# Router, token gather, expert tail and norms rebuilt in a two-block float32 kernel on one core

## What is computed

```python
def expert_choice_ffn(h, w_router, w1, w3, w2):
    cap = EC_CAPACITY_FACTOR * N // N_EXPERTS          # 32 tokens for each of 16 experts
    aff = jax.nn.softmax((h @ w_router).astype(jnp.float32), axis=-1)
    gate, idx = lax.top_k(jnp.swapaxes(aff, 1, 2), cap)
    xg = h[bidx, idx]
    ye = jnp.einsum('becf,efd->becd', jax.nn.silu(a) * b, w2) * gate[..., None]   # a, b = xg @ w1, xg @ w3
    return jnp.zeros_like(h).at[bidx, idx].add(ye)

hx2 = modulate(rmsnorm(x, norm_ffn_g[l]), ada_x[3], ada_x[4])
x = x + ada_x[5][:, None, :] * expert_choice_ffn(hx2, w_router[l], w_exp1[l], w_exp3[l], w_exp2[l])
return rmsnorm(x, final_norm_g)                        # the second block starts with a norm of this
```

## Time and profile before

| | us |
|---|---|
| median of 3 runs (lowest 2255.99, highest 2257.81) | 2257.02 |
| the profiled execution's own time | 2254.84 |
| its span, first to last instruction | 2253.0 |
| PE busy | 1889.1 |
| VectorE busy | 744.3 |
| ScalarE busy | 334.6 |
| PE starts expert 0 | 414.81 |
| PE starts the last expert's last tile | 1319.93 |
| PE starts `in0_0` of the second block | 1341.29 |

### The profile page before, as it was taken

One profiled execution on the slowest core, in us unless ns is written; L12 is line 12 of the kernel. 1 busy time (PEld: TensorE's weight loads), 2 busy tenths in 40 slices (PEclk: granted clock), 3 DMA queues, 4 the chain that ended last, 5 costly groups with the idle time before them and its releaser, 6 DMA issues.

```text
span 2253.0 us, 29442 instructions
## 1 busy us (share of the span) xinstructions
PE 1889.1 (84%) x12382; PEld 1264.7 (56%) x12382; DVE 744.3 (33%) x1716; ACT 334.6 (15%) x759; POOL 0.2 (0%) x4
## 2 busy tenths in 40 slices
...
GB/s 327 114 210 239 224 254 357 405 428 428 428 429 428 429 428 428 428 428 428 428 428 429 428 377 168 186 75 164 230 168 183 186 179 183 76 168 241 152 169 57
DMA packets 148022, 648.82 MB, mean 288 GB/s; under 512 B 10660, under 2 KB 17425, under 8 KB 123158
## 3 DMA queue, kind: packets, MB, share of 16 engines
...
HBM read 646.36 MB, written 1.05 MB: 287 GB/s over the span
## 4 chain that ended last, share of the span: by engine, by line
PE 59%; DMA 33%; DVE 4%; ACT 2%; issue 1%; SPq 0%; ACTq 0%; DVEq 0%
DMA ring<-in_w_exp 33%; PE bank L2086 15%; PE bank L922 13%; PE bank L2769 6%; PE bank L1869 4%; PE bank L1606 4%; PE bank L2684 3%; PE bank L1884 2%; PE bank L936 1%; PE bank L965 1%; PE bank L800 1%; PE bank L1533 1%; DVE scr L2595 1%; PE bank L963 1%; PE bank L451 1%
## 5 line engine op out<-in xcount | busy, mean ns | idle before, releaser
L1869 PE MATMUL bank<-ring,arena 128*32 128x512 f32 x1968 | 305.2, 754 | 207.9 <-DMA ring<-in_w_exp 197.5
L1869 PEld LDWEIGHTS bank<-ring,arena 128*32 128x32 f32 x1968 | 60.9, 124 | 433.4 <-DMA ring<-in_w_exp 313.5
L922 PE MATMUL bank<-hx,ring 128*128 128x256 f32 x1344 | 293.0, 379 | 0.7 <-ACT hx L818 0.7
L922 PEld LDWEIGHTS bank<-hx,ring 128*128 128x128 f32 x1344 | 254.6, 190 | 37.5 <-issue 3.4
L1884 PE MATMUL bank<-ring,arena 128*32 128x512 f32 x1008 | 161.0, 781 | 78.9 <-DMA ring<-in_w_exp 67.9
L1927 DVE COPY arena<-bank 128x256 f32<-128x256 f32 x16 | 6.8, 425 | 527.2 <-PE bank L1874 527.2
L2086 PE MATMUL bank<-arena 128*128 128x256 f32 x672 | 151.0, 379 | 0.2 <-DVE arena L2135 0.2
L1884 PEld LDWEIGHTS bank<-ring,arena 128*32 128x32 f32 x1008 | 32.9, 132 | 188.7 <-DMA ring<-in_w_exp 107.8
L2086 PEld LDWEIGHTS bank<-arena 128*128 128x128 f32 x672 | 127.0, 190 | 17.5 <-DVE arena L2135 0.6
L1934 DVE COPY arena<-bank 128x256 f32<-128x256 f32 x16 | 6.8, 424 | 344.6 <-PE bank L1758 344.6
L2086 PE MATMUL bank<-ring,hx 128*128 128x256 f32 x448 | 105.8, 379 | 0.0
...
## 6 DMA issues: line engine op xcount, KB each, us to landing
ring<-in_w_exp SPq DMA_DIRECT2D x186, 2048.0 KB, 16.3
...
```

The costliest lines, as they stand in the source:

```text
L922: ins = pe.matmul(b[:, o:o + n], w[:, k, j * P:(j + 1) * P], h[:, k, :], start=k == 0, stop=k == KD - 1)
L1869: ins = pe.matmul(banks[s][32 * j:32 * j + 32, :], e_xe[:, 2 * t + kk, :], w[:, kk, 512 * j:512 * j + 512], start=t + kk == 0, stop=t + kk ...
```

## The change

1. **Four more later tiles on VectorE**: 6, 8, 10 and 12 join 0 to 5 (two within Hyena, two within the mLSTM heads).
2. **late-2 and late-1 leave the router.** All pairs move down: layer one of the second block now has -2 (behind `in0_0`), -1 (within attention), 0 (behind attention), 1 (in the norm); layer two has 2 to 5 alike, with 2 in its first norm. No pair stands in the join.
3. **Router.** Logits are taken from `xT` with the gain multiplied into `w_router`, half of them within `mixout`; the token's scale is applied later, to 16 logits and to the turned rows. The token's sum of squares comes from matmuls that use the squares as weights and move 2 columns of ones; VectorE adds six of the eight blocks first. `pe_rope` and the shift's part move into `mixout`.
4. **Gather.** `e_htok` is now the weights (128 columns, every second element) and `e_ps` moves, so that the result is already turned; copy and turn go. VectorE adds the shift on the way to `e_xe`.
5. **Expert 0's tiles.** 4 to 7, 10 and 11 are in the extra places, 0 to 3 in the ring, 8 and 9 follow as 0 and 1 are used, and expert 1's first four as 2, 3, 8 and 9 are used.
6. **The last expert** leaves the loop: no gather, its last tile in two halves, each half of `y` copied as it is done, and `x moe` by pairs as the scatter goes on.
7. **Join and norms**: the sum of squares is per token (weights: squares; two columns of ones move), root and reciprocal are of 128x2, and a diagonal matrix brings the scale back over partitions (`pe_scale`). For the final norm of block one the squares are folded to two blocks, and it is done after `in0_0` (`pe_fin`).

```diff
-    tiles("late-2_", later[16:18])
-    tiles("late-1_", later[18:20])
...
+        tiles2(f"late{g}_", later[20 + 2 * g:22 + 2 * g] if g < 0 else late[2 * g:2 * g + 2])
...
-    ON_DVE = 6
+    ON_DVE = (0, 1, 2, 3, 4, 5, 6, 8, 10, 12)
     later_acc = [arena[:, 14368 + 512 * i:14880 + 512 * i].rearrange("p (a b) -> p a b", a=2) for i in range(2)]
     later_acc += [hcx[:, 2 * i:2 * i + 2, 0:N] for i in range(4)]
+    later_acc += [later_acc[2 + n // 2] for n in range(8)]
...
+    def pe_late(pe, g, between=None):
...
+            if between and i == 0:
+                between(pe)
...
         def pe_norm(pe):
             PE.stage("norm")
             b = bank(pe, key)
             for k in range(KD):
                 pe.wait_ge(*at(f"{key} square{k}"))
-                ins = pe.matmul(b[:, 0:n], ones[:, 0:P], sq[:, k, :], start=k == 0, stop=k == KD - 1)
+                for c in range(NC):
+                    ins = pe.matmul(b[:, 2 * c:2 * c + 2], sq[:, k, c * P:(c + 1) * P], ones[:, 0:2], start=k + c == 0, stop=True,
+                                    skip_group_check=True)
             ins.then_inc(*PE.step(f"full {key}"))
 
-        def act_squares(act):
+        def pe_scale(pe):
+            stage = PE.cur
+            PE.stage("norm")
+            b = bank(pe, f"{key} scale")
+            for c in range(NC):
+                pe.wait_ge(*at(f"{key} diagonal{c}"))
+                ins = pe.matmul(b[:, c * P:(c + 1) * P], ones[:, 0:P], n_diag[:, c, :], start=True, stop=True)
+            ins.then_inc(*PE.step(f"full {key} scale"))
...
+            act.activation(n_root, bank_of(key)[:, 0:4:2], ACT.Sqrt, bias=n_eps, scale=1.0 / D).then_inc(
...
+            v.reciprocal(n_rs, n_root).then_inc(*DV.step())
             v.wait_ge(*DV.last())
+            for c in range(NC):
+                v.tensor_scalar(n_diag[:, c, :], ident[:, :], n_rs[:, c:c + 1], None, ALU.mult).then_inc(
+                    *DV.step(f"{key} diagonal{c}"))
...
+    def pe_fin(pe):
+        PE.stage("join")
+        pe.wait_ge(*at("fin squares"))
+        b = bank(pe, "join x")
+        for k in range(2):
+            ins = pe.matmul(b[:, 0:N], ones[:, 0:P], sqx[:, k, :], start=k == 0, stop=k == 1)
+        ins.then_inc(*PE.step("full join x"))
...
+            if h in (0, 2):
+                dve_later_sum(v, 10 + h, 0)
+                dve_later_sum(v, 10 + h, 1)
...
+            dve_later_sum(v, 6 + 2 * o, 0)
+            dve_later_sum(v, 6 + 2 * o, 1)
...
+    EXTRA = [(4, view(arena, 0, P, TILE)), (5, view(arena, 4096, P, TILE)), (6, view(arena, 8192, P, TILE)),
+             (7, view(arena, 12288, P, TILE)), (10, mg[:, :]), (11, scr[:, :])]
     extra_of = dict(EXTRA)
-    ring_of = {t: N_PRE + m for m, t in enumerate((5, 6, 7, 8, 10, 11))}
+    ring_of = {t: N_PRE + m for m, t in enumerate((0, 1, 2, 3, 8, 9))}
...
+        elif j == 1:
+            pe_rope(pe)
+        elif j == 5:
+            pe_route_logits(pe, 0)
...
     def pe_gather(pe, name):
 
-        for c in range(NC):
-            for j in range(4):
-                ins = pe.matmul(banks[2][32 * j:32 * j + 32, 0:256], e_ps[:, c, :], e_htok[:, c, 256 * j:256 * j + 256],
-                                    start=c == 0, stop=c == NC - 1)
+        for t in range(4):
+            for kk in range(2):
+                o = banks[2][:, (2 * t + kk) * CAP:(2 * t + kk + 1) * CAP]
+                for c in range(NC):
+                    ins = pe.matmul(o, e_htok[:, c, 256 * t + kk:256 * (t + 1):2], e_ps[:, c, :], start=c == 0, stop=c == NC - 1)
         ins.then_inc(*PE.step(f"{name}gathered"))
 
-    def pe_gather_turn(pe, name):
-
-        for kk in range(2):
-            ins = pe.transpose(banks[2][:, 256 + kk * P:256 + (kk + 1) * P], e_gx[:, kk::2], ident[:, :])
-        ins.then_inc(*PE.step(f"{name}turned"))
+    def dve_gathered(v, name):
+
+        v.wait_ge(*at(f"{name}gathered"))
+        v.tensor_tensor(e_xe, banks[2][:, 0:256].rearrange("p (k s) -> p k s", k=KD), spread(e_shp, 2, CAP), ALU.add).then_inc(
+            *DV.step(f"{name}xe"))
...
+                if last and t == 3:
+                    pe.wait_ge(K.sem("tile_half"), 16)
+                    w = place(EXP0 + 11, P, 4, D)
+                else:
+                    w = tile(8 + t, 4, D)
                 for half in range(2):
+                    if last and t == 3 and half:
+                        tile(11, 4, D)
...
+                pe.wait_ge(*at("last G"))
+                for j in range(KD):
+                    pe.wait_ge(*at(f"last y{j // 4}"))
+                    ins = pe.matmul(banks[4 + j // 2][:, (j % 2) * N:(j % 2 + 1) * N], e_y[:, j * P:(j + 1) * P], e_G,
+                                        start=False, stop=True, skip_group_check=True)
+                    ins.then_inc(*PE.step(f"last scattered{j}"))
+                return
...
+                if l == 0 and t == 0:
+                    pe_fin(pe)
+                    pe_late(pe, 4 * l - 2)
+                    PE.stage("second")
...
+        pe_late(pe, 4 * l - 1)
...
         sp.wait_ge(*at("z2"))
-        extra_tile(0)
-        extra_tile(1)
+        extra_tile(4)
+        extra_tile(5)
         sp.wait_ge(*at("full merge07"))
-        one(N_PRE - 4, stream[N_PRE - 4])
-        one(N_PRE - 3, stream[N_PRE - 3])
-        extra_tile(2)
-        extra_tile(3)
+        extra_tile(6)
+        extra_tile(7)
         sp.wait_ge(*at("merged0 done7"))
-        extra_tile(4)
-        one(N_PRE - 2, stream[N_PRE - 2])
-        one(N_PRE - 1, stream[N_PRE - 1])
-        for t in (5, 6):
+        extra_tile(10)
+        for t in (0, 1, 2, 3):
             sp.wait_ge(*at(f"used {ring_of[t] - RING}"))
             expert_tile(ring_of[t], 0, t)
-        sp.wait_ge(*at("h ffn0 done"))
-        extra_tile(9)
-        for t in (7, 8):
-            sp.wait_ge(*at(f"used {ring_of[t] - RING}"))
-            expert_tile(ring_of[t], 0, t)
+        sp.wait_ge(*at("full token sums"))
+        extra_tile(11)
         K.turn = 0
-        for t, old in ((10, 5), (11, 6)):
+        for t, old in ((8, 0), (9, 1)):
             sp.wait_ge(*at(f"expert used{old}"))
             expert_tile(ring_of[t], 0, t)
-        for t, old in enumerate((7, 8, 10, 11)):
+        for t, old in enumerate((2, 3, 8, 9)):
...
+        sp.dma_start(place(n, P, 4, D)[:, :, 0:512], w[:, :, 0:512]).then_inc(K.sem("tile_half"), 16)
+        sp.dma_start(place(n, P, 4, D)[:, :, 512:1024], w[:, :, 512:1024]).then_inc(tile_sem(n), 16)
...
```

500 lines of the change are left out of this document (314 added, 186 removed).

## The result

The changed kernel takes 2263.67 us (median of 12 runs, 2259.62 to 2268.61) against 2256.11 for the kernel before (12 runs, 2254.61 to 2259.26) on the same chip: ratio 1.0031, 95% interval 1.0023 to 1.0039. It is slower by 7.6 us; 2241.2 was forecast, with 0.05 on this side. The profiled execution took 2264.78, its span is 2262.7. PE is busy 1957.0 us, 68 more than before, though four tiles of `w_ada` have gone from it to VectorE.

A forecast was written before the change was run, and what follows sets the result against it. DMA of expert weights sets the experts' pace; most of the rest is PE. Gains of 11.0 us up to expert 0, 2.6 stream and 9.9 tail, less 7.7 second block, make 15.8: 2241.2 us, range 2236 to 2247.

The forecast's parts named there:

- Step 3: Expert weight stream: the last half starts 902.5 us after expert 0's start, a gain of 2.6 us.
- the gather starves the ring: Expert loop: DMA runs dry if gather and scatter exceed 14 us; 12 us of gather would give 2271; chance 0.05.
- Step 2: Router chain from the end of `mixout` to expert 0: 19 us; expert 0 starts at 403.8, 11 us earlier.
- Step 1: First block: four later tiles on VectorE and earlier branch tiles bring the merges 5.6 us earlier (bounds 3.0 and 7).
- The 4.36 us: PE's wait in front of the merges in the kernel before, read as the landing of both branch tiles.
- Both tiles land near 323.5: First block: both branch tiles land near 323.5, so PE starts the merges about 325 instead of 330.6.
- the dry stretch: Early expert stream: expert 0 takes 35 us, so DMA is dry for some 6 us; without it, 5 us earlier.
- Step 4: Tail from the landing of the last half to `in0_0`: 11.5 us instead of 21.4, about 10 us less.
- Step 5: Second block, from `in0_0` to the end of the span: 7.7 us longer (bounds +5 and +13).
- The stage of `in0`: Second block, behind `in0_0`: the unhidden late pair adds 3.70 us and `pe_fin` 0.9.
- Attention: Second block: a late pair in each attention costs 1 us (bounds 0 and 3.7), plus 0.4 for each turn.
- The norms: Second block: the token layout is worth 0, as the late pair fills PE's gap; +0.3 us for three norms.

The follow-up runs named there:

- experiments 1 and 2: 1: the changed kernel with the loop's gather in its old form, 2255.32 us; 2: the changed kernel with its gathers moving 128 columns instead of 32, 2252.20 us.
- the wide kernel: The changed kernel with both gathers, three norms (ScalarE's table loaded ahead) and the join moving 128 columns: 2246.16 us, ratio 0.9953; again 2247.16, 0.9963.
- old norms: The wide kernel with the second block's three norms in their old form: 2245.76 us, ratio 0.9948.
- experiment 8: The changed kernel once more, 2266.19 us, ratio 1.0041; beside it the changed kernel with the join's first sum moving 128 columns, 2264.75, ratio 1.0040.
- thin pairs: Late pairs cut to one of eight row blocks: the changed kernel's two in attention, 2262.30 us; the wide kernel's three in the second block, 2243.89 us.

## Why the prediction was wrong

**Step 3, the stream: it failed, and by the largest sum.** The price of the gather was right as far as the row went: 3.96 to 4.0 us at the full clock, 4.5 taken. What I did not price was the clock: gather and scatter were to take 4.5 + 3.8 = 8.3 us a pass, and they take 11.1 in the mean and 12.9 in the pass shown. I had the clock's mean in the loop in view (0.82) and took it for a property of the stretch; in fact it changes between its two levels several times a pass. The old gather, 256 columns moved, was short at either (at most 1.95), with 3.7 to 4.1 for the scatter behind it. The new one takes 7.04 where it begins at the lower level, brings the clock down in most other passes, and leaves the scatter at 5.1 to 6.6. 902.5 us were forecast for the stream, and it takes 902.0 to 902.3 in five profiles without a narrow gather in the loop (experiments 1 and 2, the wide kernel twice, with old norms once), 903.9 and 904.3 in the other two, and 909.5 to 916.2 in every one that has it.

The rival *the gather starves the ring* named this mechanism and gave it 0.05. Its limit was too high: 14 us for gather and scatter together, counted from the end of tile 11. In the pass shown they are 12.9 and DMA already runs short. The four tiles asked for cover 19.6 us from the landing of tile 11, which PE starts at once (489.05) and ends 2.8 us later. Counted from there the limit is 11.3. That this is the reason for the difference was worked out, not tested.

**Step 2, the router: right in its sum.** `mixout` ends at 387.1 and expert 0 starts 19.1 us later; 19 was forecast, with a gather of 4.5 where it took 5.8 at the falling clock. So the rest of the chain was 1.2 us shorter than counted, and that the sum came out is luck. The 2.4 us by which expert 0 is late come from Step 1: `mixout` was to end at 384.8.

**Step 1, the first block: half right.** Merges 2.1 us earlier instead of 5.6. In the changed kernels they start between 327.4 and 329.0, and at 331.0 with the four tiles back on PE. The 4.36 us were the landing of a branch tile, as I read them, but of the second one. I followed only the first, `branch_hy`, which was issued at 309.16 instead of 316.17. The second, `branch_ml`, takes the slot of tile later13, which is still PE's, and was issued only 2.3 us earlier (first the changed kernel, then the kernel before):

```profile
315.66 0.37 SPq L3297 DMA_DIRECT2D ring<-in_w_branch_ml  x1
```

```profile
317.92 0.37 SPq L3106 DMA_DIRECT2D ring<-in_w_branch_ml  x1
```

It took 12.8 and 12.6 us to land, at 328.5 and 330.5, and the merges start at 328.50 and 330.60. In every profile they start within 0.2 us of that landing; with the four tiles back on PE it was issued at 317.88, landed at 330.9, and they started at 331.01. "Both tiles land near 323.5" is the step that failed here.

**Step 3, the dry stretch:** expert 0 took 37.8 us and not 35, for its first four tiles took 9.65 at the low clock instead of 7.07, and DMA was short in 440 to 448 (152 GB/s). It was there, as forecast.

**Step 4, the tail: right,** 11.6 against 11.5. In the second profile of the changed kernel (experiment 8) it is 13.3, with the last scatter at 4.8 instead of 3.7.

**Step 5, the second block: +18.4 instead of +7.7.** Three terms were off.
- The stage of `in0`, 8.0 instead of 4.6: the pair 3.70 and `pe_fin` 1.03 as forecast, 1.9 for `in0_0` at the low clock (15.88 against 13.97), and 1.6 of PE waiting for VectorE, which waited for a tile issued late (rows below, changed kernel). The last is a wait that I did not look for, though I had the ring's order in hand.
- Attention, 2.0 and 2.3 instead of 1.4 each: within my bounds, an error of size; PE's part of it is 1.1 and 1.6 to 2.3 by the two runs with thin pairs.
- The norms, 2.0 to 2.3 each instead of 0.1. I was right that the late pair fills the gap and that the shorter chain is worth nothing; the run with old norms beside wide ones shows it. I was wrong that it costs nothing: clock 1.1, table load 0.5. I had counted the table load nowhere, since before it lay beside the sum.

```profile
1332.61 15.88 PE L960 MATMUL bank<-ring,hx 128*128 128x512 f32 x32 [1.21 <-ACT hx L896]
...
1360.60 1.23 DVE L2296 TENSOR_TENSOR arena<-ring 128x1024 f32<-128x1024 f32 x1 [3.43 <-DMA ring<-in_w_in]
...
1363.44 1.97 PE L2266 MATMUL bank<-arena,hx 128*128 128x256 f32 x8 [1.62 <-DVE scr L2335]
```

The Trainium skill (TensorE: Matmul & The Clock Gate, HAM oscillation — how this bites in real kernels) has the clock fall when TensorE waits for data. The trace agrees for the pass shown above, in which PE had waited 2.96 us for its tile and the clock was 0.50 from 492 to 503. At the norm it does not: PE had no wait from 1559.84 on, and the clock fell to 0.50 behind the sum all the same, so there the measurement decides.
